# Latent roots from sums over a matrix of ones, key copies on ScalarE, and a modulation tile through TensorE

## The reference, cut to what matters

```python
sh1, sc1, g1, sh2, sc2, g2 = split(silu(c) @ w_mod + b_mod, 6)      # 1024 -> 6 x 1024
hx = rmsnorm(x, g) * (1 + sc1) + sh1
hc = rmsnorm(ctx, g) * (1 + csc1) + csh1                            # 256 context tokens
pq, pkv = split(hx @ w_in)                                          # the same for hc, keys only
q_m = rmsnorm(pq[:384], q_a_g) @ w_uq                               # 8 heads of 64 + 32 (rope)
kv  = rmsnorm(pkv[:256], kv_a_g) @ w_ukv                            # k_nope and v of 8 heads
k_m = concat(k_nope, rope(pkv[256:288]) broadcast to 8 heads)
o_mla = softmax(q_m k_m^T / sqrt(96)) v                             # 512 keys
o_na  = neighbourhood attention over na_q, na_k, na_v with a bias   # 8 heads of 64
x = x + g1 * (concat(o_mla, o_na) @ w_out)
x = x + g2 * moe(modulate(rmsnorm(x), sh2, sc2))                    # 16 experts, top 2 of 4 in one group
x = second_block(rmsnorm(x))                                        # gating, attention, conv FFN
```

## Time and profile before

| | |
|---|---|
| time, median of 3 runs | 755.22 us (754.8 to 755.56) |
| profiled execution, its own time | 754.42 us |
| its span, first to last instruction | 752.6 us |
| mean granted TensorE clock | 0.995 |
| TensorE / VectorE / ScalarE / GpSimd busy | 96% / 60% / 44% / 11% |
| shares of the chain of work that ended last | TensorE 69%; VectorE 12%; DMA 11%; ScalarE 5% |

### The profile page before, as it was taken

One profiled execution on the slowest core, in us unless ns is written; L12 is line 12 of the kernel. 1 busy time (PEld: TensorE's weight loads), 2 busy tenths in 40 slices (PEclk: granted clock), 3 DMA queues, 4 the chain that ended last, 5 costly groups with the idle time before them and its releaser, 6 DMA issues.

```text
span 752.6 us, 10903 instructions
## 1 busy us (share of the span) xinstructions
PE 720.6 (96%) x4136; PEld 502.5 (67%) x4140; DVE 452.0 (60%) x775; ACT 329.8 (44%) x586; POOL 83.4 (11%) x86
## 2 busy tenths in 40 slices
PE   7899997999998999999999999999999999999997
PEld 3597886655795343453354346877889888888885
DVE  1597698899556221221221148877768999998543
ACT  2474212587534101011110136655657777777433
POOL 0000041043000000000000000040000344434000
PEclk9999999999999999999999999999999999999999
DMA  9995669726178999999999997305304455495101
GB/s 376 398 387 239 245 233 387 281 75 261 29 300 319 392 421 430 427 415 427 428 428 422 420 427 282 112 1 220 145 1 173 172 215 197 152 427 228 57 1 56
DMA packets 21258, 199.50 MB, mean 265 GB/s; under 512 B 2368, under 2 KB 2880, under 8 KB 4832
## 3 DMA queue, kind: packets, MB, share of 16 engines
q1 hardware_dynamic: 20304, 195.35, 64.8%
q0 software_dynamic: 624, 3.28, 1.3%
q10 hardware_dynamic: 288, 0.30, 0.1%
HBM read 197.86 MB, written 1.05 MB: 264 GB/s over the span
## 4 chain that ended last, share of the span: by engine, by line
PE 69%; DVE 12%; DMA 11%; ACT 5%; issue 2%; POOL 1%; SPq 0%; ACTq 0%; DVEq 0%; POOLq 0%
PE banks L1779 12%; PE banks L2048 10%; PE banks L2090 8%; PE banks L1337 6%; PE banks L1816 6%; DMA ring<-in_w_up 5%; PE banks L2052 5%; DMA ring<-in_w_col 3%; DVE w_lo L2139 2%; PE banks L1734 2%; DMA ring<-in_w_mod 2%; PE banks L1582 2%; PE banks L1583 2%; PE banks L1584 2%; DVE nmax L2333 2%; PE banks L1720 2%
## 5 line engine op out<-in xcount | busy, mean ns | idle before, releaser
L2139 DVE TENSOR_TENSOR w_lo<-ring,w_hi 128x1024 fp32r<-128x1024 f32 (+1 forms) x123 | 147.3, 1204 | 57.2 <-ACT w_hi L1195 24.1
L1779 PE MATMUL banks<-ring,att 128*64 128x512 f32 x448 | 112.9, 593 | 2.6 <-DMA ring<-in_w_up 2.6
L2048 PE MATMUL banks<-h_both,w_hi 128*128 128x512 f32 x320 | 80.1, 392 | 0.0
L1779 PEld LDWEIGHTS banks<-ring,att 128*64 128x64 f32 x448 | 37.6, 137 | 61.2 <-issue 54.6
L886 ACT ACTIVATE w_hi<-ring 128x1024 fp32r<-128x1024 f32 x50 | 52.0, 1053 | 30.3 <-PE banks L1337 19.7
L2048 PEld LDWEIGHTS banks<-h_both,w_hi 128*128 128x128 f32 x320 | 57.6, 189 | 10.3
L2553 DVE TENSOR_TENSOR front<-front,banks 128x512 f32<-128x512 f32 x8 | 5.5, 688 | 95.3 <-PE banks L1779 95.3
L1190 ACT ACTIVATE w_hi<-ring 128x1024 fp32r<-128x1024 f32 x44 | 46.2, 1051 | 8.3 <-PE banks L2074 4.5
L2052 PEld LDWEIGHTS banks<-h_both,w_lo 128*128 128x128 f32 x320 | 43.7, 190 | 3.1
L2052 PE MATMUL banks<-h_both,w_lo 128*128 128x256 f32 x320 | 44.6, 282 | 0.0
L2526 DVE SCALAR_TENSOR_TENSOR ysb_lo<-banks,slot_w,ysb_hi 128x512 fp32r<-128x512 f32 x16 | 12.0, 751 | 52.2 <-ACT ysb_hi L1088 28.9
(11 more groups left out here) (391 smaller groups left out, 1532.3 us busy)
## 6 DMA issues: line engine op xcount, KB each, us to landing
ring<-in_w_up SPq DMA_DIRECT2D x21, 2048.0 KB, 9.7
ring<-in_w_down SPq DMA_DIRECT2D x9, 2048.0 KB, 12.6
ring<-in_w_in SPq DMA_DIRECT2D x8, 2048.0 KB, 18.6
ring<-in_w_gate SPq DMA_DIRECT2D x8, 2048.0 KB, 15.0
ring<-in_w_col SPq DMA_DIRECT2D x13, 1024.0 KB, 5.2
ring<-in_w_up SPq DMA_DIRECT2D x12, 1024.0 KB, 8.0
ring<-in_w_down SPq DMA_DIRECT2D x9, 1024.0 KB, 14.0
ring<-in_w_out SPq DMA_DIRECT2D x4, 2048.0 KB, 7.7
```

Of the source, the lines that this page charges most:

```text
L1779: last = nc.tensor.matmul(bank[2 + j][CAP * e:CAP * (e + 1), :], xs[:, k, at:at + CAP], gate_or_up(n + e, k, odd), start=(k == (4 if turne ...
L2048: nc.tensor.matmul(dst.rearrange("p (a t) -> p a t", a=2), granule(w_hi, j, g)[:, k, :], h2_both[:, :, k, :], start=(k == 0), stop=False, ...
L2139: return V.tensor_tensor(dst, src, high.bitcast(F32), ALU.subtract)
```

## The change

Three things change, and the line numbers shift by some.

1. `latent_sums` multiplies by a full matrix of ones: three products of 256 columns into bank 4, two of 512 into bank 5, which give the sums on all partitions at once. The roots and reciprocals are made on `rq` (128 x 256) and `rkv` (128 x 512) in SBUF, and the five scalings follow at n = 12. `latent_spread` is gone. SyncE waits for the second count of `lat_ss` before it loads over the squares.
2. The four copies of the rotated key part are ScalarE's, at n = 16 ahead of its move of `nav` 0.
3. Of the 32 column blocks 28 stay. The last 512 columns of `w_mod` are a fifth tile (`L_MOD2`) in slot 5, loaded when block 27 has been summed. TensorE streams it in step 9 of the attention into bank 7, ScalarE copies it out in step 10, TensorE picks it in step 12, and VectorE adds its bias in step 14. The second tile of `w_out` uses slot 5 afterwards and is loaded when the stream is done.

The diff, cut to its core:

```diff
-N_COL = 32
+N_COL = 28
 COL_BLOCKS = (0, 1, N_COL - 1) + tuple(range(2, N_COL - 1))
 COL_LOADS = (("A", 0, 2), ("A", 2, 1), ("4a", 3, 2), ("4b", 5, 2), ("A", 7, 2), ("4a", 9, 2), ("4b", 11, 2), ("4a", 13, 2),
-             ("4b", 15, 2), ("4a", 17, 2), ("4b", 19, 2), ("4a", 21, 2), ("4b", 23, 2), ("5a", 25, 2), ("5b", 27, 2),
-             ("5a", 29, 2), ("5b", 31, 1))
+             ("4b", 15, 2), ("4a", 17, 2), ("4b", 19, 2), ("4a", 21, 2), ("4b", 23, 2), ("5a", 25, 2), ("5b", 27, 1))
 COL_ADDED = {9: range(0, 3), 10: range(3, 6), 11: range(6, 9), 12: range(9, 12), 13: range(12, 15), 15: range(15, 21),
-             17: range(21, 28), 21: (28,), 28: (29,), 30: (30,), 32: (31,)}
+             17: range(21, 28)}
...
+        rq = mixT[:, 0, :]
+        rkv = mixT[:, 2:4, :].rearrange("p a t -> p (a t)")
+        modp2 = mixT[:, 6:8, :].rearrange("p a t -> p (a t)")
...
+            if n == L_MOD2:
+                return mod_streamed, 5
...
-            sp.wait_ge(lat_ss, 1)
+            sp.wait_ge(lat_ss, 2)
...
-            for m in (15, 16):
-                sp.wait_ge(col_sum, COL_LOADS[m - 1][1])
-                column_loads(m)
+            sp.wait_ge(col_sum, N_COL)
+            issue(L_MOD2, w_mod[4])
...
-            sp.wait_ge(col_sum, N_COL)
-            issue(L_OUT + 1, w_out[1])
             sp.wait_ge(*through(last_in_slot(L_MOE + 1)))
             for j in (1, 3):
                 expert_load(0, j)
+            sp.wait_ge(*through(L_MOD2))
+            issue(L_OUT + 1, w_out[1])
...
-            pool.wait_ge(shifted_lo, 2 * KD)
-            pool.wait_ge(kr_done, 1)
-            for h in range(4):
-                nc.gpsimd.tensor_copy(kT[rope_rows(h), h:H:4, :],
-                                      kr[rope_rows(h), :].unsqueeze(1).broadcast_to([32, 2, 512]))
...
-                    act.wait_ge(var, LAT_STEP + 1)
-                    nc.scalar.activation(rs[:, 0:6], rs[:, 0:6], ACT.Sqrt).then_inc(std, 1)
+                    act.wait_ge(var, LAT_STEP + 2)
+                    nc.scalar.activation(rq, rq, ACT.Sqrt).then_inc(std, 1)
+                    nc.scalar.activation(rkv, rkv, ACT.Sqrt).then_inc(std, 1)
...
+                    act.wait_ge(shifted_lo, 2 * KD)
+                    act.wait_ge(kr_done, 1)
+                    for h in range(4):
+                        rows = slice(32 * rope_group(h), 32 * rope_group(h) + 32)
+                        ins = nc.scalar.activation(kT[rows, h:H:4, :], kr[rows, :].unsqueeze(1).broadcast_to([32, 2, 512]),
+                                                   ACT.Copy)
+                    ins.then_inc(kr_spread, 1)
...
+                if s == STREAM_AT + 1:
+                    act.wait_ge(mod_streamed, 5)
+                    nc.scalar.activation(modp2, bank[7], ACT.Copy).then_inc(mod_copied, 1)
...
-                for j in range(6):
-                    first, n, width = (0, 3, T) if j < 2 else (768, 2, 2 * T)
-                    for k in range(n):
-                        at = first + k * width + P * (j if j < 2 else j - 2)
-                        last = nc.tensor.matmul(bank[4][:, j:j + 1], attf[:, at:at + P], ones[:, 0:1],
-                                                start=(k == 0), stop=(k == n - 1))
+                for k in range(3):
+                    last = nc.tensor.matmul(bank[4][:, 0:T], ones, attf[:, k * T:(k + 1) * T],
+                                            start=(k == 0), stop=(k == 2))
                 last.then_inc(lat_ss, 1)
-
-            def latent_spread():
-                pe.wait_ge(inv, INV_LAT + 1)
-                for j in range(6):
-                    dst = bank[4][:, j * P:(j + 1) * P] if j < 2 else bank[5][:, (j - 2) * P:(j - 1) * P]
-                    last = nc.tensor.matmul(dst, rs[:, j:j + 1].broadcast_to([P, P]), ident, start=True, stop=True)
+                for k in range(2):
+                    last = nc.tensor.matmul(bank[5][:, :], ones, attf[:, 768 + 512 * k:1280 + 512 * k],
+                                            start=(k == 0), stop=(k == 1))
                 last.then_inc(lat_ss, 1)
...
+                if s == STREAM_AT:
+                    mod_stream(L_MOD2, 7)
+                if s == PICK_AT:
+                    pe.wait_ge(mod_copied, 3)
+                    for t in range(4):
+                        last = nc.tensor.matmul(bank[7][:, 4 * t:4 * t + 4], modp2[:, t * P:(t + 1) * P], pick4,
+                                                start=True, stop=True)
+                    last.then_inc(mod_picked, 1)
...
-                    dve.wait_ge(lat_ss, 1)
-                    V.tensor_scalar(rs[:, 0:2], bank[4][:, 0:2], 1.0 / QL, EPS, ALU.mult, ALU.add)
-                    V.tensor_scalar(rs[:, 2:6], bank[4][:, 2:6], 1.0 / KVL, EPS, ALU.mult, ALU.add).then_inc(var, 1)
-                    dve.wait_ge(std, LAT_STEP + 1)
-                    V.reciprocal(rs[:, 0:6], rs[:, 0:6]).then_inc(inv, 1)
-                if n == N_BEFORE_LAT + 2:
                     dve.wait_ge(lat_ss, 2)
+                    V.tensor_scalar(rq, bank[4][:, 0:T], 1.0 / QL, EPS, ALU.mult, ALU.add).then_inc(var, 1)
+                    V.tensor_scalar(rkv, bank[5][:, :], 1.0 / KVL, EPS, ALU.mult, ALU.add).then_inc(var, 1)
+                    dve.wait_ge(std, LAT_STEP + 2)
+                    link(V.reciprocal(rq, rq))
+                    link(V.reciprocal(rkv, rkv))
                     dve.wait_ge(prod_a, copied(PROD, KVL_FIRST + 1)[1])
                     for k in range(3):
-                        V.scalar_tensor_tensor(qlat[:, k, :], qlat[:, k, :], v_("g_qa", k), bank[4][:, 0:T], ALU.mult, ALU.mult
+                        V.scalar_tensor_tensor(qlat[:, k, :], qlat[:, k, :], v_("g_qa", k), rq, ALU.mult, ALU.mult
                                                ).then_inc(lat_done, 1)
                     for k in range(2):
-                        V.scalar_tensor_tensor(kvlat[:, k, :], kvlat[:, k, :], v_("g_kva", k), bank[5][:, :], ALU.mult, ALU.mult
+                        V.scalar_tensor_tensor(kvlat[:, k, :], kvlat[:, k, :], v_("g_kva", k), rkv, ALU.mult, ALU.mult
...
+            def last_of_mod():
+                dve.wait_ge(mod_picked, 3)
+                link(V.tensor_tensor(mod[:, 44:48, 0:1], bank[7][:, 0:16].rearrange("p (t n) -> p t n", n=4)[:, :, 0:1],
+                                     v_("b_mod", 44, 4).unsqueeze(2), ALU.add))
+
             for s in range(LAST + 3):
+                if s == PICK_AT + 2:
+                    last_of_mod()
```

More of the change, by code:

```diff
@@ L543, in block_pair_kernel @@
         NORM_BANK = [7, 7, 0, 7]
[L544 to L545 removed]
+        NORM_STEP, SUMMED, NORMED, SQUARED = [0, 4, 5, 7], [0, None, 2, 4], [0, None, 16, 24], [None, None, 0, 8]
+        LAT_STEP, LN_STEP, ROW_STEP = 2, 6, 8
         SQ_LAT, SQ_TOK, SQ_ROW = 2, 3, 9
[L547 removed]
+        INV_TOK, INV_2, INV_ROW = 0, 1, 2
         TAIL = 4
```

28 lines of the change are left out of this document (11 added, 17 removed).

## The result

| | before | after |
|---|---|---|
| time, median (lowest to highest) | 755.4 us (750.99 to 757.74), 19 runs | 756.74 us (755.56 to 758.79), 19 runs |
| ratio, 95% interval | | 1.0024 [1.0013, 1.0035] |
| profiled execution; its span | 754.42; 752.6 us | 755.76; 753.9 us |
| mean granted TensorE clock | 0.995 | 0.994 |

The change costs 1.3 us, in the medians and in the spans of the profiled executions. Engine shares hardly move: TensorE 96%, VectorE 60%, ScalarE 44%, GpSimd 10% (11% before). Where the time comes from is read at three marks: the start of VectorE's move of the second `ur` product, the start of the first maximum of the attention (unit 0), and the start of the last output product beside which the attention still runs.

The account below looks back on a forecast made before the run. TensorE is busy 96% of the span, but VectorE's chain of column sums and loads sets when it passes `rotq`. +0.5 us there and +0.9 in the attention make +1.4: 756.6 us from a median of 755.22, range 752.8 to 759.8.

Parts of the forecast that it names:

- The latent roots on VectorE: In the latent norm, wide sums, roots, reciprocals and scalings take 9.6 us on VectorE, starting its next split about 4 us late.
- rival 5: Counted among the outcomes slower than 756.7 us; the prediction as given has no description or separate chance for it.
- Almost all of the 4 us are won back: Along the column loads, dropped contention and moved scalings recover the late start, leaving +0.5 us at the `ur` move.
- the walk: Step-by-step timing of column sums and loads up to the `ur` move: 125.9 us before, 126.3 to 126.4 with the change.
- TensorE's savings: In the latent norm, TensorE is ready for `rotq` about 2.9 us earlier, less new waits; none of it on the path.
- The new TensorE wait near 96: In the first `nav` product, TensorE waits about 2 us for VectorE's second split, which it can afford.
- Clock after the ones products: After the latent sums, wide products keep TensorE's clock up, at 1.00 in 78 to 84 us, worth -1.6 us.
- Stream and picks: In the attention, TensorE's 2.8 us of added work less 1.75 us of idle time lengthens it; taken as +0.9 us.
- Four sums behind `ur` and the load order: At 127 to 141 us, four sums of 1.15 us removed are worth nothing; the moved `w_out` load is hidden.
- Rival 2: At `rotq`, the low clock level falls inside TensorE's wait, returning 1.7 us: -0.3 us, 754.9 us; chance 0.16.
- Rival 1: Behind TensorE's longer `rotq` wait, one more low-clock stretch, +1.7 us; with attention hiding nothing +5.2, 760.4 us; chance 0.14.
- Rival 4: In the latent norm, wide reciprocals are cheap or their columns fit elsewhere: -2.7 us, 752.5 us; chance 0.11.

Follow-up runs that it names:

- e4: Kernel after with the two reciprocals over only 2 and 4 columns, so its latents are wrong; median 750.32 us, ratio to before 0.9941.
- e5: Kernel before with only the key copies moved to ScalarE (old latent norm, 32 column blocks, no stream); median 753.64 us, ratio to before 0.9983.
- e1: Kernel after with the old latent norm (one-column products, six-column roots and reciprocals, spreads) put back; median 754.79 us, ratio to before 0.9999.
- e2: Kernel after with the four key copies back on GpSimd; median 757.64 us, ratio to before 1.0038.
- e6: Kernel after with the four picks in step 15 instead of 12; median 755.86 us, ratio to before 1.0012.
- e3: Kernel after with all 32 column blocks on VectorE, no stream, no picks, load order as before; median 756.14 us, ratio to before 1.0009.
- e7: Kernel after with column blocks 23 to 27 summed behind later products instead of n = 17; median 750.56 us, ratio to before 0.9943.
- e8: Kernel after with the old latent norm, column blocks 23 to 27 summed late and picks in step 15; median 748.61 us, ratio to before 0.9936.
- e9: e8 with SyncE's first gate loads held until the scores of unit 4 are out; median 749.55 us, ratio to before 0.9932.
- e10: e5 with column blocks 23 to 31 of its 32 summed behind later products, no stream; median 757.72 us, ratio to before 1.0027.

## Why the prediction was right, and where not

The time predicted was 756.6 us, the median is 756.74; for the profiled execution 755.8 was predicted and 755.76 measured. The change was put at +1.4 us and is +1.3. The interval of the ratio is 0.8 us wide to either side, so an agreement to 0.1 us is partly luck; the marks, below, bear out the mechanism. By its steps:

- **The latent roots on VectorE: right to 0.1 us.** Reciprocals 1.75 and 3.35 us (5.0 predicted), splits done at 93.39 and 97.96 (93.3 and 97.9), load 7 at 95.70 (95.6), rope steps done at 104.38 (104.3), column 27 summed at 125.04 (124.8), `ur` out at 126.51 (126.3 to 126.4). Price by the element: e4 takes 4.75 us of them away, and 5.1 us go. By the Trainium skill (VectorE: DVE Perf Modes, First, the fixed hardware budget) the prediction had estimated 6.4 us for the pair; the trace has 5.10, so the rows' slope decided rightly, and rival 5 falls.
- **"Almost all of the 4 us are won back": right.** Loads 10, 11 and 12 leave at 106.70, 110.32 and 114.00 (106.6, 110.2, 113.9 predicted). From the `ur` move of the kernel before (125.66), copies alone give 125.11 (-0.55, e5), the stream and the missing loads with them 123.08 (-2.03, e1), and the wide roots bring 126.10 (+3.02). Some 1.7 us of the -2.03, and so of the +3.02, are the clock that did not fall in e1 at 80 us (load 7 leaves at 90.08 there, at 91.77 in e5). The smaller last load shortens the row of sums by 0.2 us at most: in e5 the last sum starts 1.33 us behind the one before it, in e1 1.14. The contention, 2.5 us of VectorE's work, was worth 0.55 to 0.7 on the path (e5, e2), near the 0.9 by which the walk moved, since only one of the slow sums releases a load that VectorE then waits for.
- **TensorE's savings.** Right in effect: none reached the path. In size the ones products took 2.6 us up to the next start and not 3.2.
- **The new TensorE wait near 96: its size right, what may follow it missed.** 2.03 us, 2 predicted. The prediction said that it could be afforded and did not ask what the clock does behind it: 0.50 in 100 to 102. The `uq` products start at 117.81 instead of 116.95, and the wait at `rotq` is 3.43 us, not about 5. In e6, where the clock did not fall behind the same stall, the wait is 4.84. The wait hides either case, so it cost nothing here.
- **Clock after the ones products: right**, 1.00 in 78 to 84 us. That the one-column products of before pull it down is not certain, though (below).
- **Stream and picks: right**, +0.99 against +0.9, and the mechanism too: TensorE's waits took in 1.7 us (1.75 predicted). The prediction made it one sum; e6 divides it, 0.72 for the picks and 0.27 for the rest. The stream of 1.92 us is nearly free and the picks of 0.95 us are not, because of where each stands.
- **Four sums behind `ur` and the load order: right**, worth nothing: from the `ur` move to the first maximum it takes 18.49 us (18.59 before), and no row of the attention waits for `w_out`.
- **Rivals.** Rival 2 (the low level falls inside the wait) is spoken against by e3: there the wait was 6.27 us, the clock fell within it, and some 3.2 us of work at 0.50 followed all the same. Rival 1 (one more low stretch) did not come in the profile of the kernel after, but it did in e1 and e2, at 1.4 us where the prediction had 1.7. Rival 4 (cheap reciprocals, 752.5) was the right counterfactual with too small a price: e4's median is 750.32. The walk had the `ur` move 4.1 us earlier than in the forecast, all of the 4.1 us that it saved on the reciprocals; e4 saved more, 4.75 us, and its move came 5.08 us earlier than after. In the spans e4 is 3.8 us below before, where the rival had 2.7; why the medians are 5 us apart is open.

What the prediction did not ask is whether the seven sums had to stand behind n = 17 at all. Late sums bring the kernel after from 756.7 to 750.6 us (e7), and with the old roots and the picks at step 15 the kernels run in 748.6 to 749.6 us (e8, e9). The intervals of the three overlap; the traces put e8 and e9 2.6 to 2.8 us below e7.

## What to carry to other kernels

Idle time on an engine is cover only for work that nothing behind it waits for: follow what the next instructions of that engine release, DMA issues above all, before you call five microseconds of new work hidden. When sums or copies that feed a chain of loads stand ahead of a move that the bounding engine waits for, try first to put them behind that move (0.7% of the span here, in one line), but walk each load that they release, as e10 shows. Small work moved onto a busy engine can cost more by its place than by its length, so look for the step in which the engine waits anyway. And before you lay a difference of 1 or 2 us between two traces to the edit, see whether a low clock or a late load came in only one of them.

## What the runs showed of the hardware

- **The low clock comes in stretches.** From the start of `rotq` to the first maximum TensorE does the same work in every kernel but e10. It takes 16.27 to 16.29 us where the clock stayed at 1.00 (e7, e8, e9), 17.8 to 18.0 with some 3 us of that work at 0.50 (before, after, e3, e4, e5, e6), and 19.35 to 19.39 with some 6 (e1, e2). The wait ahead of it does not sort them: 2.6 us (e4), 4.8 (e6) and 6.3 us (e3) are in the middle group, 2.8 and 4.3 us in the last. What decides between the two I could not settle.
- **The same instructions are followed by the low level in one trace and not in another.** A stall of TensorE of 2.03 or 2.04 us near 96 was followed by 0.50 in after, e2 and e7, and by 1.00 in e3 and e6. The 28 records of one-column products, without a gap in TensorE's work, brought 0.50 to 0.60 in a stretch of 80 to 84 us in before, e5 and e10, and 1.00 throughout in e1, e8 and e9; I know of no instruction up to 80 us in which the two groups differ. That was worth 1.5 us at load 7 (91.60 to 91.77 against 89.92 to 90.16). Executions of one kernel differ in the same way: of e5's eleven, two took 750.36 us at a mean granted clock of 0.999, the profiled one 753.84 at 0.994, the slowest 757.98 at 0.990. A mean of 0.999 is that of e8's trace, which is at 1.00 from 10 to 740 us, so these two can hardly have had a low stretch behind the one-column products or behind `rotq`. A clock seen in one trace is then no property of the kernel.
- **Loads in flight, and late ones.** Of loads 12 to 14, issued together, each full one lands 2.5 us behind the one before it (before, e5) and a halved one 1.2 to 1.3 us (e1, e2, e4, e6, e7). Some came a further 1 us or more late: load 13 of e3, load 14 of after, e9 and e10. In each of these a 16 KB packet of the instruction queue started two to three us before the load landed (121.2 us in after, landing at 123.8); e2, e4, e6 and e7 had none in that time and no late load, and in e1 one that started 0.8 us before the landing did not delay it. That the packet is the cause is not shown.
- **A column sum of 128x1024 takes 1.22 us alone and up to 2.05 us beside GpSimd's copies** (before, e2); on ScalarE the same copies leave it at 1.22.
- **Reciprocals are dear by the element**: 0.15 to 0.17, 0.19, 1.75 and 3.35 us for 2, 6, 256 and 512 columns in fp32, while ScalarE's roots of 256 and 512 take 0.42 and 0.62 us.
